# One of seven products changes its place in the order of TensorE's work (FFN of a decoder layer, one core of a Trainium2 chip)

## The chip, the cores and the metric

The kernel is one program on one core of a Trainium2 chip. Its engines are TensorE (PE, matrix products), VectorE (DVE), ScalarE (ACT), GpSimd (POOL) and SyncE (SP, which here only issues the DMAs of the weights). Each engine works through its own list of instructions in order and waits on semaphores where it needs another. The metric is the device time of one execution in microseconds (us). Lower is better.

## The reference, cut to what matters

The reference is one inference step of one decoder layer, for a prompt of 512 tokens and 8 sample tokens (520 columns together), model width 1024, all in float32:

```python
x = layer_norm(ALPHA * x + 0.5 * swiglu(x, ffn1_wg, ffn1_wu, ffn1_wd), ln1_g, ln1_b)
z = einsum('btd,de->bte', x, w_in)      # conv branch, pooling branch, gates -> m
x = layer_norm(ALPHA * x + einsum('btd,de->bte', m, w_out), ln2_g, ln2_b)
x = layer_norm(ALPHA * x + 0.5 * swiglu(x, ffn2_wg, ffn2_wu, ffn2_wd), ln3_g, ln3_b)

def swiglu(x, wg, wu, wd):
    hid = silu(x @ wg) * (x @ wu)       # 1024 -> 2816
    return hid @ wd                     # 2816 -> 1024
```

The change lies in the first half of both FFNs: `x @ wg` and `x @ wu`.

## The kernel before, in words

**Tiling.** Activations lie with channels on the 128 partitions and the 520 tokens along the free axis, in two halves of H = 260. The hidden width 2816 is 22 tiles of 128, called f = 0 to 21. For accuracy each operand is kept as a rounded high part and a remainder (`xh`, `xl`; `wh`, `wl`), and each 128x128 block of weights costs three matmuls with 260 columns: high by high, high by low, low by high (`run`, lines 1227 to 1229).

**Seven products in place of eight.** For f = 2 to 21 the gate tile and the up tile of one f are made together (a "pair"). The 2x2 block problem (two halves of the 1024 inputs, gate and up weights, two halves of the tokens) is computed with seven block products, after a Strassen-like scheme. One product (`half_product`) is 4 blocks x 3 matmuls = 12 matmuls. They are named P1, P2, Q3, Q4, Q5, P6, P7. Their weights are B11, B21, B22 (loaded) and T1, T2, T3, T4 (sums of loaded blocks, made by VectorE). Intermediate sums share PSUM banks: P1, then P6, then P7 add up in one bank (`x_bank`); Q5 and then Q3 add up in another (`z_bank`, which alternates); P2 has its own (`y_bank`). Q4 of the same pair is added to `x_bank` last of all.

**What is copied out in between.** ScalarE copies the bank after P1 (`first_p`), after Q5 (`first_q`) and after P6 (`first_u`). VectorE makes the gate of the first half of the tokens (`gate_first`, L928), the up values of the first half (`up_first`, L933) and of the second half (`up_second`, L938), which reads `x_bank` after P7. Only when `up_second` has read that bank may Q4 be added to it (`fourth` waits for `s.up2`). After Q4, ScalarE takes the sigmoid of the bank (`second_gate`, L625), VectorE multiplies (L946, L951: `hid_pair`), ScalarE rounds the hidden tile (`hid_up`) and VectorE makes its remainder (`hid_rest`, L922).

**A stretch.** The order of the work is written out by hand, one stretch for each f. Two spans of ten pairs (f = 2 to 11, and 12 to 21), each followed by the down projection of its hidden tiles, make one FFN; the kernel has two FFNs, so forty pair stretches. In a stretch of pair f, other than a span's first:

- TensorE: P1(f), Q5(f), Q4(f-1), P6(f), P2(f), Q3(f), P7(f). Q4 of the last pair of a span stands in the down projection. In a span's first stretch the order is P1, P2, Q5, P6, Q3, P7.
- ScalarE (`pair_steps`, lines 627 to 650): copy after P1; copy after Q5; round the three loaded weight blocks of pair f+1 (`round_pair`, 1536 columns); sigmoid of pair f-1; round T1 and T3 of f+1 (`round_thirteen`, 1024 columns); copy after P6; round the hidden tile of f-1; round T2 and T4 of f+1 (`round_twenty_four`); sigmoid of the first half of the gate (L650).
- VectorE (lines 973 to 991): `up_second`(f-1), `gated_first`(f-1) (L942), the weight sums of f+1 (L871, L876, L881; the last one, T4, waits until Q4(f-1) has used the slot it writes), `hid_pair`(f-1), remainder of T1 and T3 (L885, waits for ScalarE's rounding), `hid_rest`(f-1), remainder of T2 and T4 (L890), `gate_first`(f), `up_first`(f). In the first two stretches of an FFN four tiles of `scale_residual` (L1010) follow.
- GpSimd: the three remainders of the loaded blocks of f+1 (L503), when ScalarE has rounded them and T4 is made.
- SyncE issues the loads of later pairs as the slots come free (L405, L411).

All products are counted in one semaphore, `w_used`; `number` holds the place of each product in TensorE's order, and the table has to be written in that same order.

Of the kernel before, what the change touches and what calls it, by code (L numbers as in the profile page):

```python
# [55 lines left out]
def build(nc, x_prompt, x_sample, state_conv, state_pool, ln1_g, ln1_b, ffn1_wg, ffn1_wu, ffn1_wd,  # L56
# [36 lines left out]
    with ExitStack() as ctx:  # L93
# [70 lines left out]
        def pair_of(pair):  # L164
            return ps[:, 2 * pair:2 * pair + 2, 0:H]

        def two(ap):

            return ap.rearrange("p (h n) -> p h n", h=2)
# [114 lines left out]
        def counted(*what):  # L284
            number[what] = len(number) + 1

        for n in range(2):
            for j in range(4):
                counted(n, "open", j)
            for g, (f0, f1) in enumerate(SPANS):  # L290
                for f in range(f0, f1):
                    counted(n, "P1", f)
                    if f == f0:
                        counted(n, "P2", f)
                    counted(n, "Q5", f)
                    if f > f0:
                        counted(n, "Q4", f - 1)
                    counted(n, "P6", f)
                    if f > f0:
                        counted(n, "P2", f)  # L300
                    counted(n, "Q3", f)
                    counted(n, "P7", f)
                counted(n, "Q4", f1 - 1)
                for d in range(K):
                    counted(n, "down", g, d)
            if n == 0:
                for c in range(12 * G):
                    counted("mix", c)
                for d in range(K):
                    counted("out", d)  # L310
# [236 lines left out]
        def _(act):  # L547
            def copy(out, in_):
                return nc.scalar.activation(out, in_, ACT.Copy)  # L549
# [60 lines left out]
            def ffn_steps(n):  # L610
                s = ffn[n]

                def gate_opened(f):
                    act.wait_ge(w_used, number[n, "open", 2 * f])
                    nc.scalar.activation(two(gate[f]), pair_of(2 * f), ACT.Sigmoid).then_inc(s.gate_on, 1)

                def hid_up(f, pair):
                    act.wait_ge(s.hid_made, f + 1)
                    copy(two(hid_hi[:, f % HELD[0], :]), pair_of(pair)).then_inc(s.hid_round, 1)

                def second_gate(f):
                    act.wait_ge(w_used, number[n, "Q4", f])
                    if f > 2:
                        act.wait_ge(s.gated2, f - 2)
                    nc.scalar.activation(gate_on2, bank(f % 2, 1), ACT.Sigmoid).then_inc(s.on2, 1)  # L625

                def pair_steps(f, f0, weights):

                    x_bank, z_bank = bank(f % 2, 1), bank(2, f % 2)
                    act.wait_ge(w_used, number[n, "P1", f])  # L630
                    if f > 2:
                        act.wait_ge(s.gate1, f - 2)
                    copy(first_p, x_bank).then_inc(s.p_kept, 1)
                    act.wait_ge(w_used, number[n, "Q5", f])
                    if f > 2:
                        act.wait_ge(s.up2, f - 2)
                    copy(first_q, z_bank).then_inc(s.q_kept, 1)
                    weights(0)
                    if f > f0:
                        second_gate(f - 1)  # L640
                    weights(1)
                    act.wait_ge(w_used, number[n, "P6", f])
                    if f > 2:
                        act.wait_ge(s.up1, f - 2)
                    copy(first_u, x_bank).then_inc(s.u_kept, 1)
                    if f > f0:
                        hid_up(f - 1, (f - 1) % 2)
                    weights(2)
                    act.wait_ge(s.gate1, f - 1)
                    nc.scalar.activation(bank(f % 2, 0), gate_sum, ACT.Sigmoid).then_inc(s.on1, 1)  # L650

                round_form(n, 0)
                round_thirteen(n, 2)
                gate_opened(0)
                round_form(n, 1)
                round_twenty_four(n, 2)
                gate_opened(1)
                round_form(n, 2)
                round_form(n, 3)
                hid_up(0, 1)  # L660
                hid_up(1, 3)
                for g, (f0, f1) in enumerate(SPANS):
                    for f in range(f0, f1):
                        def weights(step):
                            if f + 1 < f1:
                                (round_pair, round_thirteen, round_twenty_four)[step](n, f + 1)
                            elif step < 2:
                                round_chunk((n, "down", g, step))
                        pair_steps(f, f0, weights)
                    round_chunk((n, "down", g, 2))  # L670
                    second_gate(f1 - 1)
                    hid_up(f1 - 1, (f1 - 1) % 2)
                    round_chunk((n, "down", g, 3))
                    round_chunk((n, "down", g, 4))
                    if g == 0:
                        for d in range(5, K):
                            round_chunk((n, "down", g, d))
                        round_pair(n, f1)
                        round_thirteen(n, f1)
                        round_twenty_four(n, f1)  # L680
                square_tile(2 * n, 0)
                round_chunk((n, "down", 1, 5))
                square_tile(2 * n, 1)
                square_tile(2 * n, 2)
                round_chunk((n, "down", 1, 6))
                square_tile(2 * n, 3)
                round_chunk((n, "down", 1, 7))
# [521 lines left out]
        def _(pe):  # L1209
# [166 lines left out]
            def ffn_steps(n):  # L1376
# [15 lines left out]
                def fourth(f):  # L1392
                    pe.wait_ge(t24_ready, pair_no(n, f))
                    pe.wait_ge(s.up2, f - 1)
                    half_product("Q4", "T4", f, bank(f % 2, 1), start=False)

                def second(f):
                    pe.wait_ge(lo_ready, lo_no[n, "B21", f])
                    half_product("P2", "B21", f, bank(f % 2, 0))

                def pair(f, f0):
                    y_bank, x_bank, z_bank = bank(f % 2, 0), bank(f % 2, 1), bank(2, f % 2)

                    pe.wait_ge(lo_ready, lo_no[n, "B11", f])
                    if f == 2:
                        pe.wait_ge(s.gated, 1)
                    elif f == 12:
                        pe.wait_ge(s.part, 6)
                    elif f == 13:
                        pe.wait_ge(s.part, 8)  # L1410
                    else:
                        pe.wait_ge(s.hid_ready, f - 1 if f > 3 else 1)
                    half_product("P1", "B11", f, x_bank)
                    if f == f0:
                        second(f)

                    pe.wait_ge(t13_ready, pair_no(n, f))
                    if f == 2:
                        pe.wait_ge(form_ready, 4 * n + 1)
                        pe.wait_ge(s.gated, 2)  # L1420
                    elif f == 12:
                        pe.wait_ge(s.part, 7)
                    elif f > 3:
                        pe.wait_ge(s.up1, f - 3)
                    half_product("Q5", "T1", f, z_bank)
                    if f > f0:
                        fourth(f - 1)

                    pe.wait_ge(t24_ready, pair_no(n, f))
                    if f == 2:  # L1430
                        pe.wait_ge(form_ready, 4 * n + 2)
                    pe.wait_ge(s.p_kept, f - 1)
                    half_product("P6", "T2", f, x_bank, start=False)
                    if f > f0:
                        second(f)

                    pe.wait_ge(lo_ready, lo_no[n, "B22", f])
                    if f == 2:
                        pe.wait_ge(form_ready, 4 * n + 3)
                    pe.wait_ge(s.q_kept, f - 1)  # L1440
                    half_product("Q3", "B22", f, z_bank, start=False)

                    if f == 2:
                        pe.wait_ge(form_ready, 4 * n + 4)
                    pe.wait_ge(s.u_kept, f - 1)
                    half_product("P7", "T3", f, x_bank, start=False)
# [223 lines left out]
```

## Time and profile before

| | |
|---|---|
| time, median of 3 runs | 1130.2 us (1125.5 to 1130.94) |
| the profiled execution | 1128.01 us, span 1126.2 us |
| mean granted TensorE clock | 0.979 of full |
| TensorE busy | 1070.2 us (95% of the span), 8731 matmuls |
| VectorE busy | 700.2 us (62%) |
| GpSimd busy | 514.1 us (46%) |
| ScalarE busy | 438.9 us (39%) |
| chain of work that ended last | 83% TensorE, 10% VectorE, 2% ScalarE, 2% DMA |

The span is the time from the first to the last instruction of the core. A matmul with 260 columns is shown with some 0.28 us, but they overlap: one starts about every 0.12 us. "Idle before, releaser" in a row is the time in which the engine had nothing to do before an instruction, and what ended it; "issue" means that the profile shows no releaser.

### The profile page before, as it was taken

Reading aid. Unit: us, or ns where it says so; the run is one execution under the profiler, and the core shown is the slowest. Engines: PE = TensorE matmul, PEld = TensorE weight load, DVE = VectorE, ACT = ScalarE, POOL = GpSimd, SP = SyncE. Lnnn points to the kernel's source line nnn. Section 1 sums busy time; section 2 is a strip of 40 time slices with the busy share of each in tenths; the row PEclk is TensorE's granted clock in tenths of the full one; section 3 lists DMA queues with packets and bytes.
Section 4 is the critical chain, followed back from the end, with each engine's and each line's share of the span. In section 5 each row is a group of like instructions: output and inputs, shape, how many; then the busy total and the mean of one; then the engine's idle time right before and its main releaser. Section 6 shows DMA issues by size and latency. Waiting matters only on the chain.

```text
span 1126.2 us, 20814 instructions
## 1 busy us (share of the span) xinstructions
PE 1070.2 (95%) x8731; PEld 1060.8 (94%) x8731; DVE 700.2 (62%) x1019; ACT 438.9 (39%) x658; POOL 514.1 (46%) x259
## 2 busy tenths in 40 slices
PE   8799999999999788999999999986999999999997
PEld 7799999999999787999999999986999999999996
DVE  6798830278946576353545536789986114887486
ACT  3355541155543154223232223354555222555223
POOL 4255463245564156344354444243565343655431
PEclk9999999999999888999999999998999999999998
DMA  7123344233334113233232332203333433333312
GB/s 210 56 79 110 95 112 113 76 95 113 94 95 113 51 49 112 63 93 113 80 100 76 111 95 79 75 7 88 104 103 95 113 94 89 99 95 104 103 40 76
DMA packets 195001, 103.29 MB, mean 92 GB/s; under 512 B 4420, under 2 KB 193428, under 8 KB 194901
## 3 DMA queue, kind: packets, MB, share of 16 engines
q1 hardware_dynamic: 194827, 101.85, 31.4%
q8 instruction: 69, 1.13, 0.4%
q14 instruction: 23, 0.19, 0.1%
q10 hardware_dynamic: 82, 0.12, 0.1%
HBM read 99.74 MB, written 2.48 MB: 91 GB/s over the span
## 4 chain that ended last, share of the span: by engine, by line
PE 83%; DVE 10%; issue 2%; DMA 2%; ACT 2%; POOL 0%; DVEq 0%; ACTq 0%; POOLq 0%
PE ps L1244 13%; PE ps L1247 13%; PE ps L1245 13%; PE ps L1227 13%; PE ps L1229 13%; PE ps L1228 13%; DVE x L1101 2%; DMA raw<-in_ffn_wd_dram 1%; DVE x L1082 1%; DVE xl L855 1%; DMA raw<-in_w_in_dram 1%; PE ps L1292 1%; DVE form_lo L906 1%; PE ps L1299 1%; PE ps L1293 1%
## 5 line engine op out<-in xcount | busy, mean ns | idle before, releaser
L494 POOL TENSOR_TENSOR wl<-raw,wh 128x1024 fp32r<-128x1024 f32 (+3 forms) x96 | 259.0, 2703 | 297.9 <-ACT wh L549 297.8
L549 ACT ACTIVATE wh<-raw 128x1024 fp32r<-128x1024 f32 (+3 forms) x216 | 252.7, 1171 | 225.0 <-DMA raw<-in_ffn_wd_dram 107.1
L503 POOL TENSOR_TENSOR wl<-raw,wh 128x512 fp32r<-128x512 f32 x120 | 225.4, 1906 | 236.8 <-DVE raw L881 191.0
L1227 PE MATMUL ps<-form_hi,wh 128*128 128x260 f32 x640 | 182.4, 285 | 4.8 <-ACT temps L549 4.8
L1229 PE MATMUL ps<-form_hi,wl 128*128 128x260 f32 x640 | 181.8, 284 | 0.0
L1228 PE MATMUL ps<-form_lo,wh 128*128 128x260 f32 x640 | 181.6, 284 | 0.0
L1244 PE MATMUL ps<-xh,wh 128*128 128x260 f32 x672 | 176.3, 283 | 2.5 <-DVE ymix L1175 2.5
L1245 PE MATMUL ps<-xl,wh 128*128 128x260 f32 x672 | 175.6, 283 | 0.0
L1227 PE MATMUL ps<-xh,wh 128*128 128x260 f32 x480 | 138.2, 288 | 16.1 <-DVE temps L913 12.0
L1244 PE MATMUL ps<-hid_hi,wh 128*128 128x260 f32 x544 | 141.9, 282 | 0.0
L1245 PE MATMUL ps<-hid_lo,wh 128*128 128x260 f32 x544 | 141.9, 283 | 0.0
L1228 PE MATMUL ps<-xl,wh 128*128 128x260 f32 x480 | 137.3, 286 | 0.0
L1229 PE MATMUL ps<-xh,wl 128*128 128x260 f32 x480 | 136.8, 285 | 0.0
L1247 PE MATMUL ps<-xh,wl 128*128 128x260 f32 x672 | 135.7, 283 | 0.0
L1244 PEld LDWEIGHTS ps<-xh,wh 128*128 128x128 f32 x672 | 127.5, 190 | 2.7 <-DVE ymix L1175 2.7
L1245 PEld LDWEIGHTS ps<-xl,wh 128*128 128x128 f32 x672 | 127.0, 189 | 0.0
L1227 PEld LDWEIGHTS ps<-form_hi,wh 128*128 128x128 f32 x640 | 121.1, 189 | 6.0 <-issue 4.3
L1228 PEld LDWEIGHTS ps<-form_lo,wh 128*128 128x128 f32 x640 | 121.4, 190 | 0.0
L1229 PEld LDWEIGHTS ps<-form_hi,wl 128*128 128x128 f32 x640 | 121.3, 190 | 0.0
L1247 PE MATMUL ps<-hid_hi,wl 128*128 128x260 f32 x544 | 109.5, 283 | 0.0
L1227 PEld LDWEIGHTS ps<-xh,wh 128*128 128x128 f32 x480 | 91.9, 192 | 17.9 <-issue 17.1
L1247 PEld LDWEIGHTS ps<-xh,wl 128*128 128x128 f32 x672 | 103.9, 189 | 0.0
(195 smaller groups left out, 2152.7 us busy)
## 6 DMA issues: line engine op xcount, KB each, us to landing
raw<-in_w_in_dram SPq DMA_DIRECT2D x44, 512.0 KB, 3.9
raw<-in_ffn_wg_dram SPq DMA_DIRECT2D x80, 256.0 KB, 3.3
raw<-in_ffn_wd_dram SPq DMA_DIRECT2D x16, 768.0 KB, 5.8
b<-in_ffn_wu_dram SPq DMA_DIRECT2D x40, 256.0 KB, 3.4
raw<-in_ffn_wu_dram SPq DMA_DIRECT2D x40, 256.0 KB, 3.0
raw<-in_ffn_wd_dram SPq DMA_DIRECT2D x16, 640.0 KB, 4.9
raw<-in_w_out_dram SPq DMA_DIRECT2D x8, 512.0 KB, 4.0
xrow<-in_x_prompt_dram SPq DMA_DIRECT2D x4, 512.0 KB, 5.3
```

What stands on the lines that cost most here:

```text
L494: nc.gpsimd.tensor_tensor(held(wl, what), held(raw, what), held(wh, what).bitcast(F32), ALU.subtract).then_inc(lo_ready, 1)
L503: nc.gpsimd.tensor_tensor(wl_slot[:, s, :], raw_slot[:, s, :], wh_slot[:, s, :].bitcast(F32), ALU.subtract).then_inc(lo_ready, 1)
L549: return nc.scalar.activation(out, in_, ACT.Copy)
L855: tt(xl[:, k, :], x32[:, k, :], xh[:, k, :].bitcast(F32), ALU.subtract).then_inc(x_ready, 1)
L906: tt(form_lo[:, i, :], form32[:, i, :], form_hi[:, i, :].bitcast(F32), ALU.subtract).then_inc(form_ready, 1)
L1101: ins = stt(v, v, par[:, 2 * n * K + k:2 * n * K + k + 1], rstd[:], ALU.mult, ALU.mult)
L1227: mm(out, wh[:, at, :], vh, start=start and n == 1, stop=False, skip_group_check=more)
L1228: mm(out, wh[:, at, :], vl, start=False, stop=False, skip_group_check=more)
L1229: ins = mm(out, wl[:, at, :], vh, start=False, stop=n == count, skip_group_check=more)
L1244: mm(bank(pair, h), wh[:, at, :], half(vh, h), start=start and n == 1, stop=False)
L1245: mm(bank(pair, h), wh[:, at, :], half(vl, h), start=False, stop=False)
L1247: ins = mm(bank(pair, h), wl[:, at, :], half(vh, h), start=False, stop=stop and n == count)
```

## The change

In every pair stretch except a span's first, TensorE runs Q4(f-1) straight after P1(f), and Q5(f) after it: P1, Q4, Q5, P6, P2, Q3, P7. ScalarE's sigmoid of pair f-1 stands straight after the copy of P1, ahead of the copy of Q5 and of the roundings. The table of places follows. VectorE, GpSimd and SyncE keep their lists; no instruction is added or removed.

```diff
@@ the table of places
                     counted(n, "P1", f)
                     if f == f0:
                         counted(n, "P2", f)
-                    counted(n, "Q5", f)
                     if f > f0:
                         counted(n, "Q4", f - 1)
+                    counted(n, "Q5", f)
                     counted(n, "P6", f)
@@ ScalarE, pair_steps
                     copy(first_p, x_bank).then_inc(s.p_kept, 1)
+                    if f > f0:
+                        second_gate(f - 1)
                     act.wait_ge(w_used, number[n, "Q5", f])
                     if f > 2:
                         act.wait_ge(s.up2, f - 2)
                     copy(first_q, z_bank).then_inc(s.q_kept, 1)
                     weights(0)
-                    if f > f0:
-                        second_gate(f - 1)
                     weights(1)
@@ TensorE, pair
                     half_product("P1", "B11", f, x_bank)
                     if f == f0:
                         second(f)
+                    else:
+                        fourth(f - 1)
...
                     half_product("Q5", "T1", f, z_bank)
-                    if f > f0:
-                        fourth(f - 1)
```

## Rows read from the trace of the kernel before

**Rows 1.** The page: busy time of TensorE, its share of the span, its instructions.

```profile
PE   1070.2 (95%) x8731; PEld 1060.8 (94%) x8731; DVE 700.2 (62%) x1019; ACT 438.9 (39%) x658; POOL 514.1 (46%) x259
```

**Rows 2.** Waits: who waited for whom, us in total, times, longest.

```profile
PE ps L1227 <- DVE temps L938: 3.2, 2, 1.9
```

**Rows 3.** Windows: length, busy us by engine, granted clock, DMA share, GB/s.

```profile
238.00:326.00 88.00, 88.00 (x732) 87.87 (x731) 73.29 (x102) 49.38 (x80) 49.48 (x27) 1.00 0.34 99
```

**Rows 4.** Timeline, stretches of pairs 5 and 6, TensorE: start, us, engine, line.

```profile
84.16 0.28 PE L1227 MATMUL ps<-xh,wh 128*128 128x260 f32 x1
94.25 0.28 PE L1227 MATMUL ps<-xh,wh 128*128 128x260 f32 x1
```

**Rows 5.** Timeline of the same stretches, ScalarE.

```profile
87.25 0.39 ACT L549 ACTIVATE temps<-ps 128x260 f32<-128x260 f32 x1 [1.06 <-PE ps L1229]
89.17 1.06 ACT L549 ACTIVATE wh<-raw 128x1024 fp32r<-128x1024 f32 x1
```

**Rows 6.** Timeline of the same stretches, VectorE.

```profile
88.78 0.69 DVE L881 TENSOR_TENSOR raw<-raw 128x512 f32<-128x512 f32 x1 [0.82 <-PE ps L1229]
...
90.52 1.47 DVE L885 TENSOR_TENSOR wl<-raw,wh 128x1024 fp32r<-128x1024 f32 x1
...
92.52 1.70 DVE L890 TENSOR_TENSOR wl<-raw,wh 128x1024 fp32r<-128x1024 f32 x1
...
94.82 0.41 DVE L938 TENSOR_TENSOR temps<-temps,ps 128x260 f32<-128x260 f32 x1
...
96.95 1.23 DVE L871 TENSOR_TENSOR raw<-raw,b 128x1024 f32<-128x1024 f32 x1 [1.38 <-issue]
```

**Rows 7.** Timeline of the same stretches, GpSimd and the DMA issues of SyncE.

```profile
89.61 5.76 POOL L503 TENSOR_TENSOR wl<-raw,wh 128x512 fp32r<-128x512 f32 x3 [4.03 <-DVE raw L881]
...
93.01 0.37 SPq L405 DMA_DIRECT2D raw<-in_ffn_wu_dram  x1
```

**Rows 8.** Timeline from pair 12 (a span's first stretch) into pair 13, TensorE.

```profile
228.90 0.28 PE L1227 MATMUL ps<-form_hi,wh 128*128 128x260 f32 x1
...
238.15 0.36 PE L1227 MATMUL ps<-xh,wh 128*128 128x260 f32 x1
...
239.65 0.28 PE L1227 MATMUL ps<-form_hi,wh 128*128 128x260 f32 x1
```

**Rows 9.** Timeline of pair 12: ScalarE, GpSimd, VectorE.

```profile
230.54 0.39 ACT L549 ACTIVATE temps<-ps 128x260 f32<-128x260 f32 x1 [2.49 <-PE ps L1229]
...
232.38 5.77 POOL L503 TENSOR_TENSOR wl<-raw,wh 128x512 fp32r<-128x512 f32 x3 [16.18 <-ACT wh L549]
...
233.28 1.47 DVE L885 TENSOR_TENSOR wl<-raw,wh 128x1024 fp32r<-128x1024 f32 x1 [2.64 <-ACT wh L549]
...
237.59 0.41 DVE L938 TENSOR_TENSOR temps<-temps,ps 128x260 f32<-128x260 f32 x1
```

**Rows 10.** Timeline of pairs 3 and 4, first FFN: TensorE, VectorE.

```profile
66.44 0.36 PE L1227 MATMUL ps<-xh,wh 128*128 128x260 f32 x1 [1.33 <-DVE temps L938]
...
76.90 0.35 PE L1227 MATMUL ps<-xh,wh 128*128 128x260 f32 x1
...
70.26 1.46 DVE L885 TENSOR_TENSOR wl<-raw,wh 128x1024 fp32r<-128x1024 f32 x1
...
76.34 0.41 DVE L938 TENSOR_TENSOR temps<-temps,ps 128x260 f32<-128x260 f32 x1
```

**Rows 11.** Timeline, TensorE: first matmul of P7 in the last stretches, f = 11 and 21.

```profile
154.06 0.39 PE L1227 MATMUL ps<-form_hi,wh 128*128 128x260 f32 x1 [0.27 <-ACT temps L549]
...
324.81 0.28 PE L1227 MATMUL ps<-form_hi,wh 128*128 128x260 f32 x1
```

**Rows 12.** Timeline, GpSimd and VectorE: pair 9; L890 while GpSimd is idle.

```profile
130.42 4.77 POOL L503 TENSOR_TENSOR wl<-raw,wh 128x512 fp32r<-128x512 f32 x3 [4.77 <-ACT wh L549]
...
131.78 2.27 DVE L885 TENSOR_TENSOR wl<-raw,wh 128x1024 fp32r<-128x1024 f32 x1
...
226.84 1.22 DVE L890 TENSOR_TENSOR wl<-raw,wh 128x1024 fp32r<-128x1024 f32 x1
```

## The prediction

> **What bounds the kernel now.** I read the busy shares first: TensorE is busy for 1070.2 us of 1126.2, 95% [rows 1]. Then the waits of TensorE, for where it is not fed. Of all its waits only one kind concerns the order of Q4: it waited for `up_second` (L938) twice, 3.2 us together, 1.9 at most [rows 2], both in the first stretches of an FFN. Then the windows, to see whether the pair stretches are full: from 238 to 326, nine stretches of pairs, TensorE is busy for 88.00 of 88.00 us at a granted clock of 1.00, which is its higher level, 2.4 GHz [rows 3]. So TensorE sets the pace there, and no change of order can make a full stretch shorter; it can only open a gap. The timeline gives the pace: P1 of one pair starts at 84.16, P1 of the next at 94.25, a stretch of 10.09 us, seven products of 1.44 [rows 4]. VectorE is busy for 73.29 of the 88 us: it has slack, but not much, and its list is a chain with ScalarE's. That is the resource to follow.
>
> **How near Q4 is to its wait now.** Q4(f-1) may start when `up_second`(f-1) has read the bank. In the steady stretch that instruction starts at 94.82 [rows 6]; TensorE follows it by 0.56 us where it really waits (237.59 to 238.15) [rows 8, 9]. So Q4 could start at 95.38. P1 runs from 94.25 for 1.44 us, to 95.69. In the order of before Q5 stands next, to 97.13, and Q4 has 1.75 us of slack. Put second, it wants to start at 95.69: 0.31 us of slack are left, if `up_second` stays where it is. It does not.
>
> **What is added or removed.** Nothing: the same 84 matmuls in each stretch, the same copies and sigmoids, the same DMAs. 36 products Q4 and 36 sigmoids move; four Q4 in the down projections stay.
>
> **The sigmoid and Q4, earlier.** Q4 one product earlier frees the slot of T4 earlier, for which L881 now waits 0.82 us [rows 6], and lets `hid_pair` run earlier. On TensorE this is worth nothing, since nothing there waits for them in a full stretch. The sigmoid also leaves its place between two roundings (copy of Q5 at 87.25, rounding of T1/T3 at 89.17, with the sigmoid in between) [rows 5]; that small gain is in the distance that I take below from a stretch without it. If the moved sigmoid were late it would hold the copy of Q5, but Q4 ends 1.44 us ahead of Q5.
>
> **The copy of Q5, later.** This is the cost. Q5 is now third, so it ends 1.44 us later in the stretch, and ScalarE's copy of it, with all that is queued behind that copy (rounding of the loaded blocks, of T1/T3, copy after P6, rounding of the hidden tile, of T2/T4), moves with it. VectorE's L885 waits for the rounding of T1/T3. The order "Q5 third" already exists in a span's first stretch, so I need not guess: pair 12's Q5 starts at 228.90, its copy at 230.54 (1.64 later) [rows 8, 9], and L885, which waited 2.64 us for ScalarE, at 233.28 (2.74 after the copy) [rows 9]. In the steady stretch of pair 5, Q5 would start at 84.16 + 2 x 1.44 = 87.05 and L885 at 87.05 + 1.64 + 2.74 = 91.43. Before it started at 90.52 [rows 6], so it is 0.91 later. From L885 to `up_second` VectorE works without a gap for 4.30 us (90.52 to 94.82). So `up_second` comes at 95.73 and Q4 could start at 96.29, against 95.69 wanted: TensorE stands for 0.60 us in each stretch.
>
> **The loop.** TensorE's standing does not heal it, since the copy of Q5 waits for Q5, which is behind Q4. From Q4 to the next Q4: to Q5's start 1.50 (238.15 to 239.65, after a stop) [rows 8], to the copy 1.64, to L885 2.74, to `up_second` 4.30, to Q4 0.56: 10.74, say 10.75 us. Against 10.09 that is 0.66 us for each of the loops. It holds in later stretches if VectorE is ready for L885 before the rounding is; the sums L871 to L881 and `hid_pair` end about 1.3 us before, even where L871 waits for its DMA: the block issued at 93.01 was used at 96.95, 3.94 us later [rows 6, 7], and in the new loop that puts L871 some 0.8 us behind Q4, L885's input from VectorE at about 4.6 and its start at 5.9. SyncE's issues hang on P1, P2 and Q3, which move together with TensorE.
>
> **The sum, by absolute times, first FFN.** Span of pairs 12 to 21: Q4(12) is bound by `up_second` already and starts at 238.15 in both orders, but behind it Q5 is still to come. Q4(20) follows after 8 loops: 238.15 + 8 x 10.75 = 324.15. P7(21) starts after Q5, P6, P2, Q3: 1.50 + 4 x 1.44 = 7.27 later, 331.4. Before: 324.81 [rows 11]. Loss 6.6 us. Span of pairs 2 to 11: Q4(2) waits for `up_second` and starts at 66.44 in both. Then comes a long stretch, since `scale_residual` stands ahead of `up_second`: L885 to L938 took 6.08 there [rows 10], so Q4(3) = 66.44 + 1.50 + 1.64 + 2.74 + 6.08 + 0.56 = 78.96 against 76.90. Q4(10) = 78.96 + 7 x 10.75 = 154.2, P7(11) = 161.5 against 154.06 [rows 11]. Loss 7.4 us; the small stops of before are contained in that 154.06. What follows, the down projection, is bound by TensorE and gives nothing back. The second FFN repeats both spans: 2 x (6.6 + 7.4) = 28.0 us. The profiled execution took 1128.0, so 1156.0; the median of the three runs is 2.2 above that execution, so 1158.2 by the median. I say 1157.
>
> **VectorE against GpSimd, the unsure term.** The 4.30 us contain L885 and L890 beside GpSimd's remainders, and their price hangs on how they meet. L885 took 1.47 where it started 0.91 us after GpSimd's first piece (89.61, 90.52) [rows 6, 7], and 2.27 where it started 1.36 after it [rows 12]. In the new order both hang on ScalarE alone, GpSimd on the first rounding, VectorE on the second, and pair 12 shows this case: 232.38 and 233.28, 0.90 apart, 1.47 us [rows 9]. So I take 1.47. The ends: 2.27, 0.80 more for each of 30 loops; or no meeting at all: with GpSimd idle such a remainder took 1.22 [rows 12], so L885 and L890 would take 2.44 in place of 1.47 + 1.70 [rows 6], 0.73 less, which is all of the loop's loss.
>
> The Trainium skill ("SBUF — State Buffer", Who interferes with whom) says that a VectorE instruction with two SBUF inputs and a GpSimd one that reads SBUF exclude each other for a whole instruction, by who is first. The 2.27 beside 1.47 fits that in kind; if every loop met in the bad way, by that rule the time would be that of the third rival.
>
> **Rivals.**
> 1. Not slower, 1127: `up_second` stays ahead of Q4. The mechanism: an earlier T4 and an earlier sigmoid clear VectorE's list (0.82 us of waiting in L881), which pays for the later rounding, and TensorE never stops; the small waits for ScalarE before P7 (0.27) [rows 11] go. It decides at 0.31 us: if L885 slips by less than that. For it: the slack and the idle time of VectorE. Against: L885 waited for ScalarE, not for VectorE, in the stretch that has Q5 third.
> 2. Half hidden, 1135: the loop costs nothing because the remainders run clear of GpSimd (2.44 in place of 3.17), and only the fixed losses stay, Q5 behind a bound Q4 at the head of each span: 4 x 1.44, and nearly 2 for `scale_residual`. Against: pair 12 shows them meeting.
> 3. Worse, 1181: they meet as in pair 9, 30 x 0.80 = 24 us on top of 1157. Against: the 0.90 us between them is set by two consecutive roundings of ScalarE.
> That the clock falls because of the stops I leave out: TensorE stopped for 1.33 us ahead of 66.44 [rows 10], twice the stop expected here, and its matmul distances after that are those of the full stretches.
>
> **How the numbers follow.** The loop as reckoned: 0.76. Rival 1: 0.10. Rival 2: 0.07. Rival 3: 0.07. The likeliest has its own range of about 6 us to each side (0.2 us per loop). The range 1136 to 1166 leaves out rivals 1 and 3 and the edges. Under 0.5% (5.7 us) a measurement of this kernel can hardly tell from no change; faster by more than that would need more stops removed than the pair stretches have: 0.02. Rival 1 falls within 0.5%, with a little of rival 2: 0.09. Slower: 0.89.
>
> **What would show it.** In the profile after: TensorE's wait for L938 grows from 2 times, 3.2 us to some 34 times, about 20 us and more; the distance from Q4 to Q4 is 10.75; L885 shows idle time ended by ScalarE; L881's wait for TensorE is gone; P7(21) of the first FFN starts near 324.8 + 7.4 + 6.6 = 338.8. I am wrong if TensorE is full from stretch to stretch, or if L885 starts as early as before.

## The result and the profile after

| | before | after |
|---|---|---|
| time, median | 1130.57 us (1125.5 to 1135.13, 4 runs) | 1166.94 us (1163.15 to 1168.46, 4 runs) |
| profiled execution, span | 1128.01, 1126.2 us | 1168.46, 1166.7 us |

The ratio is 1.0318, 95% interval 1.0267 to 1.0369: slower by 3.2%. The forecast was slower, 1157, range 1136 to 1166; the time lies 0.9 us above the range and 10 above the value.

The page and the waits of TensorE after, against [rows 1, 2]:

```profile
PE 1086.9 (93%) x8731; PEld 1072.9 (92%) x8731; DVE 700.0 (60%) x1019; ACT 436.6 (37%) x658; POOL 516.1 (44%) x259
```

```profile
PE ps L1227 <- DVE temps L938: 26.4, 36, 3.3
```

All 36 moved products Q4 now wait for `up_second` (L938), 26.4 us together; before it was 2 and 3.2 us. VectorE and ScalarE did the same work in the same time. TensorE is busy for 16.7 us longer with the same matmuls: a first sign that some of them ran at the lower clock.

The window over eight steady stretches after (its columns: length; busy us of TensorE, of its weight loads, of VectorE, ScalarE and GpSimd, each with its instructions; granted clock; DMA share; GB/s). For 3.55 of 86 us no matmul ran, at full clock.

```profile
248.00:334.00 86.00, 82.45 (x672) 81.16 (x672) 68.91 (x97) 44.54 (x73) 45.96 (x25) 1.00 0.31 91
```

The timeline of one steady stretch after (start us, length, engine, line), TensorE, ScalarE, GpSimd and VectorE, against [rows 4 to 7, 9]:

```profile
92.70 0.35 PE L1227 MATMUL ps<-xh,wh 128*128 128x260 f32 x1 [0.45 <-DVE temps L938]
...
103.46 0.36 PE L1227 MATMUL ps<-xh,wh 128*128 128x260 f32 x1 [0.44 <-DVE temps L938]
...
95.86 0.39 ACT L549 ACTIVATE temps<-ps 128x260 f32<-128x260 f32 x1 [1.06 <-PE ps L1229]
...
97.70 5.75 POOL L503 TENSOR_TENSOR wl<-raw,wh 128x512 fp32r<-128x512 f32 x3 [5.00 <-ACT wh L549]
...
98.60 1.47 DVE L885 TENSOR_TENSOR wl<-raw,wh 128x1024 fp32r<-128x1024 f32 x1 [1.98 <-ACT wh L549]
...
102.91 0.41 DVE L938 TENSOR_TENSOR temps<-temps,ps 128x260 f32<-128x260 f32 x1
```

From Q4 to the next Q4 it is 10.76 us. The parts: Q4 to the copy of Q5 3.16 (92.70 to 95.86), copy to L885 2.74, L885 to L938 4.31, L938 to Q4 0.55. VectorE stood idle for 1.98 us before L885, waiting for ScalarE: the chain runs Q5, ScalarE, VectorE, Q4. L885 took 1.47, 0.90 after GpSimd's start, as in pair 12 [rows 9].

**Where 40.5 us of span went.** Cut at the first matmul of each stage, from the timelines of the two profiled executions (both enter the pairs of the first FFN at 47.26):

| stage | before | after | difference | forecast |
|---|---|---|---|---|
| first FFN, pairs 2 to 11 | 108.34 | 118.71 | 10.4 | 7.4 |
| down projection, pairs 12 to 21, to the first pooling product | 281.15 | 287.78 | 6.6 | 6.6 |
| pooling product to the next input product | 9.88 | 12.14 | 2.3 | 0 |
| rest of the mixing stage and output projection | 281.43 | 281.98 | 0.5 | 0 |
| normalisation and opening of the second FFN | 39.10 | 42.24 | 3.1 | 0 |
| second FFN, pairs 2 to 11 | 106.42 | 117.18 | 10.8 | 7.4 |
| down projection, pairs 12 to 21, rest | 252.62 | 259.41 | 6.8 | 6.6 |

The head of the first FFN after: first matmul of Q4(2), Q5(3), Q4(3), Q5(4), against [rows 10]; then windows behind the two stops and in the steady part.

```profile
66.41 0.36 PE L1227 MATMUL ps<-xh,wh 128*128 128x260 f32 x1 [2.76 <-DVE temps L938]
68.20 0.42 PE L1227 MATMUL ps<-form_hi,wh 128*128 128x260 f32 x1
...
80.44 0.35 PE L1227 MATMUL ps<-xh,wh 128*128 128x260 f32 x1 [2.20 <-DVE temps L938]
82.53 0.42 PE L1227 MATMUL ps<-form_hi,wh 128*128 128x260 f32 x1
```

```profile
66.00:70.00 4.00, 3.59 (x21) 3.62 (x22) 3.79 (x7) 0.39 (x1) 0.00 (x0) 0.69 0.22 64
...
80.40:86.00 5.60, 5.56 (x34) 5.59 (x35) 3.80 (x6) 1.29 (x3) 0.00 (x0) 0.70 0.19 55
100.00:157.00 57.00, 54.64 (x446) 53.54 (x444) 46.30 (x66) 28.73 (x48) 31.98 (x17) 1.00 0.32 92
```

The reader is to see the third number from the right, the granted clock: it is 0.69 and 0.70 behind the two stops, a mix of the levels 2.4 and 1.2 GHz, and 1.00 later. Q4(2) to Q5(3) took 1.79 in place of 1.50, Q4(3) to Q5(4) 2.09. P7(21) of the first FFN was forecast near 338.8 and started at 341.85, 3.0 us later.

### The profile page after: what moved, and what is told of

Its sections match the earlier page's. It is cut to its first block, busy times and chain, and to the rows that moved or that the text cites. A ratio compares the mean times of both kernels' runs of the same rounds, so it can differ in the third digit from the quotient of the medians.

```text
span 1166.7 us, 20814 instructions
## 1 busy us (share of the span) xinstructions
PE 1086.9 (93%) x8731; PEld 1072.9 (92%) x8731; DVE 700.0 (60%) x1019; ACT 436.6 (37%) x658; POOL 516.1 (44%) x259
## 4 chain that ended last, share of the span: by engine, by line
PE 64%; DVE 22%; ACT 8%; issue 4%; DMA 1%; DVEq 0%; ACTq 0%; POOL 0%; POOLq 0%
PE ps L1244 13%; PE ps L1247 13%; PE ps L1245 13%; PE ps L1227 7%; ACT wh L549 7%; PE ps L1229 7%; PE ps L1228 7%; DVE wl L890 5%; DVE wl L885 4%; DVE x L1101 2%; DVE x L1082 1%; DVE temps L938 1%; DVE temps L928 1%; DVE temps L933 1%; DVE xl L855 1%
## 5 line engine op out<-in xcount | busy, mean ns | idle before, releaser
L503 POOL TENSOR_TENSOR wl<-raw,wh 128x512 fp32r<-128x512 f32 x120 | 228.0, 1928 | 270.9 <-ACT wh L549 205.0
L549 ACT ACTIVATE wh<-raw 128x1024 fp32r<-128x1024 f32 (+3 forms) x216 | 249.1, 1171 | 216.6 <-DMA raw<-in_ffn_wd_dram 103.4
L1244 PE MATMUL ps<-xh,wh 128*128 128x260 f32 x672 | 176.6, 284 | 4.8 <-DVE ymix L1175 4.8
L1227 PE MATMUL ps<-xh,wh 128*128 128x260 f32 x480 | 141.6, 295 | 39.1 <-DVE temps L938 26.4
```

What stands on the lines that cost most here:

```text
L503: nc.gpsimd.tensor_tensor(wl_slot[:, s, :], raw_slot[:, s, :], wh_slot[:, s, :].bitcast(F32), ALU.subtract).then_inc(lo_ready, 1)
L1227: mm(out, wh[:, at, :], vh, start=start and n == 1, stop=False, skip_group_check=more)
L1244: mm(bank(pair, h), wh[:, at, :], half(vh, h), start=start and n == 1, stop=False)
```

## The experiments

Each was timed beside the kernel before on the same chip; the median of the kernel before was 1132.74 there for the first four and 1132.29, on another chip, for the others. Each was profiled in one execution.

**1. TensorE's order alone.**

```diff
  copy(first_p, x_bank)
- if f > f0: second_gate(f - 1)
  ... copy(first_q, z_bank)
  weights(0)
+ if f > f0: second_gate(f - 1)
  weights(1)
```

> TensorE has the new order (Q4 second), ScalarE keeps the old one: the sigmoid stands between the two roundings again. Theory (the copy of Q5 and the roundings behind it set a loop Q4 to Q4 of 10.75 us): the sigmoid adds its 0.26 us to the loop, 11.0 us from Q4 to Q4 in the steady stretches, a stop of about 0.7 us of TensorE ahead of each Q4, and 30 loops x 0.26 = 8 us on top of the changed kernel, about 1175. Rival (it is the forward sigmoid that costs, by holding ScalarE's copy of Q5): back towards the time before, 1130 to 1140.

Measured: 1202.6 us, ratio 1.0649 (1.0577 to 1.0722). Steady stretch, TensorE, ScalarE, GpSimd, VectorE:

```profile
89.44 0.36 PE L1227 MATMUL ps<-xh,wh 128*128 128x260 f32 x1 [0.94 <-DVE temps L938]
...
101.44 0.36 PE L1227 MATMUL ps<-xh,wh 128*128 128x260 f32 x1 [0.93 <-DVE temps L938]
...
92.59 0.39 ACT L549 ACTIVATE temps<-ps 128x260 f32<-128x260 f32 x1 [3.24 <-PE ps L1229]
...
94.25 0.38 ACT L625 ACTIVATE temps<-ps 128x260 f32<-128x260 f32 x1
...
94.43 4.77 POOL L503 TENSOR_TENSOR wl<-raw,wh 128x512 fp32r<-128x512 f32 x3 [7.23 <-ACT wh L549]
...
94.66 0.43 DVE L946 TENSOR_TENSOR ps<-temps,ps 128x260 f32<-128x260 f32 x1 [2.44 <-ACT temps L625]
...
95.80 2.27 DVE L885 TENSOR_TENSOR wl<-raw,wh 128x1024 fp32r<-128x1024 f32 x1
```

The loop is 12.00, not 11.0. The direction was right and the size wrong, for two reasons. The late sigmoid holds `hid_pair` (L946), which stands ahead of L885 on VectorE: L885 starts 3.21 us after the copy of Q5 (92.59 to 95.80), not 2.74. And it then starts 1.37 us after GpSimd's first remainder and takes 2.27, not 1.47, so L885 to L938 is 5.08, not 4.31. Together 0.47 + 0.77 = 1.24, which is 12.00 - 10.76. So the forward sigmoid is no burden: beside this order of TensorE it saves 36 us.

The head of this run shows something else. Its Q4(2) waited longer than in the changed kernel, and the clock did not fall behind that stop:

```profile
64.08 0.36 PE L1227 MATMUL ps<-xh,wh 128*128 128x260 f32 x1 [3.33 <-DVE temps L938]
...
64.00:68.00 4.00, 3.92 (x33) 3.95 (x33) 2.79 (x4) 0.77 (x2) 0.00 (x0) 1.00 0.02 5
```

Nor did it behind the next one (2.30 us ahead of 77.44).

**2. ScalarE's order alone.**

```diff
  copy(first_p, x_bank)
+ if f > f0: second_gate(f - 1)
  ... copy(first_q, z_bank)
  weights(0)
- if f > f0: second_gate(f - 1)
  weights(1)
```

> TensorE keeps the old order (Q4 third), ScalarE has the new one: the sigmoid ahead of the copy of Q5, so that copy waits for Q4 and comes about 1.7 us later. Theory: VectorE's L885 comes 1.2 us later in the stretch, up_second too, but Q4 stands third and has 1.75 us of slack, so TensorE stays full; loss only in the second stretch of each FFN, about 1 us each: 1131 to 1133. Rival (a later copy and later roundings cost by themselves, wherever Q4 stands): some 15 us or more, 1145 and up.

Measured: 1131.85 us, ratio 0.9987 (0.9945 to 1.0028), as the theory said. The copy of Q5 and all behind it came later, L885 waited for ScalarE, and in the steady stretches nothing was lost:

```profile
92.75 1.47 DVE L885 TENSOR_TENSOR wl<-raw,wh 128x1024 fp32r<-128x1024 f32 x1 [1.09 <-ACT wh L549]
...
97.06 0.41 DVE L938 TENSOR_TENSOR temps<-temps,ps 128x260 f32<-128x260 f32 x1
```

P1 of this stretch started at 95.30, so `up_second` came 1.76 us behind it, where it came 0.57 behind it before (94.25 and 94.82) [rows 4, 6]. That is 1.19 us later, and the slack of Q4 in third place was 1.75. A late `up_second` costs only what exceeds the slack of the product that waits for it.

**3. The rounding ahead of the copy of Q5.**

```diff
  if f > f0: second_gate(f - 1)
+ weights(0)
  ... copy(first_q, z_bank)
- weights(0)
  weights(1)
```

> The changed kernel, but ScalarE rounds the three loaded blocks before it waits for Q5 and copies it. Theory: L885 comes 1.4 us earlier against Q5, about as early as in the kernel before, and the steady stretches are full again (10.09 us, no stop before Q4). What stays is the head of each span, Q5 behind a Q4 that is bound: about 1.4 us in the spans of pairs 12 to 21 and 3 in those of pairs 2 to 11, two of each: about 1139 and not over 1145. Rival (the new place of Q4 is itself too early for VectorE's chain): stops of 0.4 us or more stay in every stretch, 1150 to 1160.

Measured: 1133.44 us, ratio 1.0030 (0.9992 to 1.0067). The stops of the steady stretches are gone. A window over seven of them:

```profile
78.00:150.00 72.00, 72.00 (x602) 72.00 (x601) 59.19 (x86) 39.12 (x65) 40.55 (x21) 1.00 0.36 103
```

With Q4 second on TensorE and only the place of one rounding changed on ScalarE, 33 of the 36 us are back. This shows the cause of the steady loss: the work that stands behind the copy of Q5. How L885 meets GpSimd changed too (1.18 us behind GpSimd's start, and it took 1.23), but L885 to L938 was 4.20 in place of 4.31, so that is worth 0.11 of the 0.67 us of a loop. I had expected 1139. The head of pairs 12 to 21 cost nothing, since the rounding is earlier in the first stretch of the span too. The heads of pairs 2 to 11 still cost something: Q4(2) waited 3.32 us, and the ten pairs took 110.88 and 109.99 us in the two FFNs, against 108.34 and 106.42 before.

**4. The changed kernel with `scale_residual` spread.**

```diff
  hid_pair(f - 1)
+ if 3 <= f <= 10: scale_residual(2 * n, range(f - 3, f - 2))
  rest_thirteen(n, f + 1)
...
- if f in (2, 3):
-     scale_residual(2 * n, range((f - 2) * HK, (f - 1) * HK))
```

> The changed kernel, but the eight tiles of scale_residual (L1010) stand one each in the stretches of pairs 3 to 10, behind hid_pair, where VectorE is idle for 1.98 us, and no longer ahead of up_second in the first two stretches. Theory: the two long stops of TensorE (2.8 and 2.2 us; 3.3 and 2.2 in the second FFN), after which the matmuls run at half their pace for some 3.5 us, go; Q4(3) starts at about 74.3 and Q4(4) at 85.0 in place of 80.44 and 92.70; the loops of 10.76 stay. 7 to 8 us less in each FFN: 1150 to 1153. The granted clock from 66 to 86 us is 1.00. Rival (the pace is low there for a reason other than the stops, or VectorE's tiles lengthen each loop): the dips of the clock stay, or the distance from Q4 to Q4 grows by up to 0.75 us: 1160 and more.

Measured: 1149.73 us, ratio 1.0173 (1.0106 to 1.024). Q4(3) and Q4(4):

```profile
74.80 0.36 PE L1227 MATMUL ps<-xh,wh 128*128 128x260 f32 x1 [0.57 <-DVE temps L938]
...
85.57 0.35 PE L1227 MATMUL ps<-xh,wh 128*128 128x260 f32 x1 [0.43 <-DVE temps L938]
```

The theory held: 10.77 us from Q4 to Q4 from the start, no long stop, and a granted clock of 1.00 from 66 to 86 us.

**5. The kernel before with `scale_residual` spread** (as in 4, but ahead of `weight_sums(n, f + 1)`).

> The kernel before (old order on both engines), with one tile of scale_residual in each of the stretches of pairs 3 to 10, ahead of the weight sums, in place of four each in the stretches of pairs 2 and 3. Theory: up_second comes in time in the first two stretches, TensorE's waits for L938 (3.2 us) go, and every other stretch keeps its 10.09 us, since L885 hangs on ScalarE and up_second has 1.75 us of slack for the added 0.76: 2 to 5 us less than before, about 1129 beside a before of 1132. Rival (VectorE's chain is too tight for it): stops in the stretches of pairs 3 to 10, 1135 or more.

Measured: 1126.19 us, ratio 0.9943 (0.9913 to 0.9973), 12 runs of it beside 23 of the kernel before. TensorE has no wait for L938 left, and pairs 2 to 11 take 105.05 and 104.06 us in the two FFNs, against 108.34 and 106.42. By the ratios this is 0.6% under the kernel before (a small gain, but the interval ends below 1) and 3.6% under the changed one.

**6. The first stretch with a Q4 in the old order.**

```diff
- if f > f0:           # Q4(f-1) second, sigmoid forward
+ if f > f0 + 1:       # in the table, on ScalarE and on TensorE
...
+ if f == f0 + 1:      # Q4(f-1) third, sigmoid between the roundings
```

> The changed kernel, but the first stretch with a Q4 in each span (pairs 3 and 13) keeps the old order on both engines. Theory: the head losses shrink (Q4(3) at about 76.9 in place of 80.44, Q4(4) at 87.7 in place of 92.70, and 2 us in the spans of pairs 12 to 21), the loops of 10.76 stay: about 14 us less than the changed kernel, 1153. Rival (the order in the head does not matter, only the steady stretches do): within 3 us of the changed kernel, 1164 and more.

Measured: 1150.57 us, ratio 1.0176 (1.0127 to 1.0226). Q4(2), Q4(3), Q4(4), with the line numbers of this kernel:

```profile
63.87 0.36 PE L1231 MATMUL ps<-xh,wh 128*128 128x260 f32 x1 [1.91 <-DVE temps L942]
...
74.34 0.36 PE L1231 MATMUL ps<-xh,wh 128*128 128x260 f32 x1 [1.56 <-DVE temps L942]
...
85.10 0.36 PE L1231 MATMUL ps<-xh,wh 128*128 128x260 f32 x1 [0.43 <-DVE temps L942]
```

This execution reached the pair stretches some 2.5 us earlier, so the distances count: 10.47 and 10.76, where the changed kernel has 14.03 and 12.26. That is 5.1 us less in the head of the first FFN. Four of the 36 places of Q4 hold 16 of the 36 us. In the second FFN Q4(2) waited 1.90 us, the granted clock fell behind it, and the first distance was 11.15.

**7. Both mends on the changed kernel.**

```diff
+ weights(0)            # ahead of the copy of Q5, as in 3
+ scale_residual(...)   # one tile behind hid_pair, as in 4
```

> Both mends on the changed kernel: ScalarE rounds the loaded blocks ahead of the copy of Q5, and scale_residual is spread one tile to a stretch behind hid_pair. Theory: no stop ahead of any Q4 over 0.5 us, pair stretches of 10.09, some 2.5 us less in each FFN than the kernel before: about 1127 beside a before of 1132, the same as the old order with the same spreading. Rival (Q4 second brings something of its own, since hid_pair and T4 come earlier): 3 us or more under the old order with the spreading.

Measured: 1138.23 us, ratio 1.0069 (1.0038 to 1.01): neither 1127 nor less. GpSimd and VectorE in a stretch of pairs 3 to 10:

```profile
86.99 4.98 POOL L503 TENSOR_TENSOR wl<-raw,wh 128x512 fp32r<-128x512 f32 x3 [5.79 <-ACT wh L549]
...
87.26 1.31 DVE L1010 TENSOR_SCALAR x<-x 128x520 f32<-128x520 f32 x1
88.50 2.32 DVE L885 TENSOR_TENSOR wl<-raw,wh 128x1024 fp32r<-128x1024 f32 x1
```

The added tile meets GpSimd (1.31 us, where it took 0.42 in experiment 4) and pushes L885 to 1.51 us behind GpSimd's start, where it takes 2.32. Q4 stops again, and these stretches last 10.76 us. The stretches of pairs 13 to 20, which got no tile, have L885 at 1.23 us and last 10.09, so it is the tile. Pairs 2 to 11 take 111.50 and 109.86 us in the two FFNs, 12.3 us more than in experiment 5; the medians of the two lie 12.0 apart. The profiled execution was the fastest of its twelve (1129.12): parts of it where no tile stands were short, above all from the first pooling product to the end of the output projection (289.81 us, 294.16 in experiment 5) and ahead of the first FFN's pairs (45.28, 48.09).

**8. The stops filled.**

```diff
  def fourth(f):
+     if f in (2, 3):
+         pe.wait_ge(s.hid_ready, 2)
+         for _ in range((18, 14)[f - 2]):
+             nc.tensor.transpose(ps[:, 7, 0:P], ident[:], ident[:])
```

> The changed kernel with 18 and 14 idle transposes into an unused bank ahead of Q4(2) and Q4(3) of each FFN: TensorE has something to do during the two long stops, nothing waits for them. Theory (the pace halves behind the stops because TensorE stood still): Q4 to Q5 is 1.50 us in both places (1.79 and 2.09 now), Q4(3) at about 78.9 and Q4(4) at 89.7, granted clock 1.00 from 66 to 86 us, and 6.5 us less in all, 1160. Rival (the low pace there has another cause, such as where the DMAs or the other engines stand): the distances and the time stay as in the changed kernel, 1167.

Measured: 1162.18 us, ratio 1.0274 (1.022 to 1.0328). Q4(2), Q5(3), Q4(3), Q5(4), Q4(4), and the window over both:

```profile
67.08 0.36 PE L1227 MATMUL ps<-xh,wh 128*128 128x260 f32 x1 [0.77 <-DVE temps L938]
68.58 0.28 PE L1227 MATMUL ps<-form_hi,wh 128*128 128x260 f32 x1
...
79.62 0.36 PE L1227 MATMUL ps<-xh,wh 128*128 128x260 f32 x1 [0.68 <-DVE temps L938]
81.13 0.28 PE L1227 MATMUL ps<-form_hi,wh 128*128 128x260 f32 x1
...
90.37 0.36 PE L1227 MATMUL ps<-xh,wh 128*128 128x260 f32 x1 [0.44 <-DVE temps L938]
```

```profile
66.00:86.00 20.00, 18.55 (x154) 18.13 (x153) 15.73 (x26) 9.20 (x15) 7.15 (x5) 1.00 0.26 77
```

Q4 still waits for the same instruction, but the clock is 1.00, Q4 to Q5 takes 1.50 and 1.51, and the distances are 12.54 and 10.75 in place of 14.03 and 12.26: 1.5 us back at each stop. In the second FFN the distances are 12.53 and 10.75, in place of 14.05 and 12.27. So standing still was what brought the lower clock: behind the four long stops of the changed kernel it fell each time, behind the same four with something to do in them it never did. But it does not bring it each time, as experiment 1 shows. By medians the filling is worth 4.8 us (6.5 expected), near the spread of the runs; the distances are what shows it.

## Why the prediction was right in kind and too low

- **Direction and mechanism: right.** Q4 became bound by `up_second`, through Q5, ScalarE's roundings and L885. Experiment 3 undid it by one place in ScalarE's list, and 2 showed that a delay of `up_second` of 1.19 us is free while Q4 stands third.
- **The loop: right in size.** 10.75 forecast, 10.76 measured, term by term. Taking the distance from a span's first stretch, which already had Q5 third, gave 2.74 and 1.47 exactly. The spans of pairs 12 to 21 lost 6.6 and 6.8, forecast 6.6.
- **The head of each FFN: the step that failed.** The forecast left the clock out of its sum: "That the clock falls because of the stops I leave out: TensorE stopped for 1.33 us ahead of 66.44 [rows 10], twice the stop expected here". That compared the clock only with the steady stop. In the head the same sum made stops of 2.8 and 2.4 us (measured 2.76 and 2.20), which I never wrote down as stops. Behind each the clock fell, so Q5 ended 1.5 us later and its copy came 1.5 us later (Q4 to that copy was 4.64 us, 66.41 to 71.05, in place of 3.16), and since the loop hangs on that copy, the loss stayed. So Q4(3) was at 80.44, not 78.96, and Q4(4) 12.26 behind it, not 10.75. That is 3.0 us in the first FFN and 3.4 in the second (3.1 of it in the same two distances): 6.4 of the 12.5 us missing between 28.0 and 40.5. Experiments 4 and 8 showed it from both sides: without the stops, and with the stops filled, the clock was 1.00.
- **The trace before had the warning.** In pair 2 TensorE stopped for as long as the sum said of Q4(2), and the clock fell behind it:

```profile
56.15 0.36 PE L1227 MATMUL ps<-form_hi,wh 128*128 128x260 f32 x1 [2.75 <-ACT temps L549]
...
56.00:60.00 4.00, 3.85 (x22) 3.88 (x23) 3.93 (x5) 3.88 (x6) 0.82 (x1) 0.67 0.00 0
```

  In experiment 5 the same stop (2.76 us ahead of 56.98) had no fall behind it. So the right term would have been a chance, not a certainty. Over the ten profiled executions 14 stops of 1.89 to 3.33 us stand ahead of a Q4. The clock fell behind nine of them: all four of the changed kernel, both in experiment 3, one of four in experiment 1, the one in experiment 2, one of two in experiment 6, and not behind the 1.9 us of the kernel before. The longest without a fall was 3.33 us and the shortest with one 1.89, so no length found here divides them; behind the stops of 1.56 us and less ahead of a Q4 it never fell. Why some stops are followed by a fall and others of the same length are not stays open.
- **The rest of the 40.5, 5.9 us, lies in stages where the edit changes no instruction** (2.3 + 0.5 + 3.1 in the table). The two stages, before and after, and the same in experiment 5 (columns as in rows 3):

```profile
436.75:446.63 9.88, 7.35 (x63) 7.14 (x61) 9.71 (x11) 5.49 (x7) 8.57 (x4) 0.99 0.81 234
728.06:767.16 39.10, 27.46 (x227) 26.14 (x225) 33.42 (x46) 21.99 (x37) 18.58 (x11) 0.96 0.12 34
```

```profile
453.75:465.89 12.14, 7.34 (x63) 7.13 (x61) 11.97 (x11) 5.60 (x8) 11.11 (x5) 0.90 0.75 207
747.87:790.11 42.24, 31.43 (x227) 30.38 (x225) 33.40 (x46) 22.00 (x37) 18.55 (x11) 0.85 0.11 31
```

```profile
434.56:446.72 12.16, 7.35 (x62) 7.14 (x60) 11.97 (x11) 5.62 (x8) 11.02 (x5) 0.90 0.75 208
728.72:767.82 39.10, 27.43 (x227) 26.11 (x225) 33.42 (x46) 22.00 (x37) 18.58 (x11) 0.97 0.12 34
```

  The first stage is 12.16 in experiment 5, which is faster than the kernel before, and 12.15 in experiment 2, which is the same; the second is 42.26 in experiment 2 and 39.10 in 5. So both lengths occur in kernels that are as fast as the one before, and the profiled execution of before had the short ones. That they differ from execution to execution of one kernel is inferred, since each kernel was profiled once. By medians the loss is 36.4, by the pair stretches of the two traces 34.6. Against the forecast of 1157 the median is 9.9 higher: 6.4 are the heads of the FFNs (6.1 of it with the clock), 1.2 is that I took 1157 and not the 1158.2 of the sum, 0.4 that the median of before is 1130.57 and not 1130.2, and 1.9 stay unplaced.
- **The sigmoid: under-priced in words, right in the sum.** I called its forward place "that small gain". Experiment 1 put 1.24 us for each loop on it, without which the change would have cost 70 us. The sum held because I took its distances from a stretch in which no sigmoid stands between the roundings. I did not see that a late sigmoid holds `hid_pair`, ahead of L885.
- **The rivals.** The third did not happen in the changed kernel, but its price is real: L885 took 2.27 and 2.32 in experiments 1 and 7. Of the 0.73 us of the second, experiment 3 shows 0.11.

## What to carry to other kernels

Before a product is moved forward, walk the loop from its last input back through every in-order list until the loop meets the product itself, and take the distances from a place in the trace that already has the new order. Write down each stop that the sum creates and its length. Where the trace has a stop of that length with the lower clock behind it, give the sum two values, with the fall and without it (here 1.5 us for each stop), and let the range hold both. When a tile of work is moved to an idle gap of VectorE, look at where the next instruction then meets GpSimd.

## What the runs showed of the hardware

- After stops of TensorE of 2.76 and 2.20 us in the changed kernel the granted clock was 0.69 and 0.70 over windows of 4.0 and 5.6 us, and each cost 1.5 us beyond the stop. After 3.33 us in experiment 1 and 1.91 us in experiment 6 it stayed 1.00, and after 1.89 us in experiment 2 and 1.90 us in experiment 6 it fell. With idle transposes in the stop it stayed 1.00.
- The same VectorE subtraction of 1024 columns took 1.22 us alone, 1.47 when it began 0.90 us after GpSimd's first remainder (34 stretches of the changed kernel), 1.23 at 1.18 us (experiment 3), 2.27 at 1.37 us (32 stretches of experiment 1) and 2.32 at 1.51 us (experiment 7). Starting later can mean ending later by more than the delay. By these rows what decides is whether it begins before or after GpSimd's second remainder, shown here in experiment 1, where VectorE's L885 began at 95.80, and in the changed kernel, where it began at 98.60:

```profile
95.69 1.30 POOL L503 TENSOR_TENSOR wl<-raw,wh 128x512 fp32r<-128x512 f32 x1
...
98.94 2.28 POOL L503 TENSOR_TENSOR wl<-raw,wh 128x512 fp32r<-128x512 f32 x1
```

  In the first row GpSimd began 0.11 us earlier and kept its 1.30, and VectorE took 2.27. In the second row VectorE began 0.34 us earlier and took 1.47, and GpSimd 2.28. That fits the exclusion that the Trainium skill describes ("SBUF — State Buffer", Who interferes with whom).
